# A Conformer block in one fp32 kernel: LayerNorm and the last two channel chunks by token halves, and weights' loads issued from ScalarE

## The reference, cut to what matters

```python
def conformer_conv_module(h, w_pw1, b_pw1, w_dw, b_dw, ln_g, ln_b, w_pw2, b_pw2):
    a, g = jnp.split(h @ w_pw1 + b_pw1, 2, axis=-1)
    u = a * jax.nn.sigmoid(g)
    u = causal_depthwise_conv(u, w_dw) + b_dw        # 31 taps over tokens, per channel
    u = jax.nn.silu(layer_norm(u, ln_g, ln_b))       # mean and variance over the 1024 channels
    return u @ w_pw2 + b_pw2
...
h = h + rms_norm(m, norm_mix_post[layer])
```

## Time and profile before

| | us |
|---|---|
| median of 3 runs | 2382.27 (2381.09 to 2384.25) |
| the profiled execution's own time | 2383.93 |
| its span in the profile | 2382.1 |
| TensorE busy | 2320.1 |
| VectorE busy | 1330.0 |
| ScalarE busy | 875.6 |
| mean granted TensorE clock | 0.992 of 2.4 GHz |

### The profile page before, as it was taken

How to read it: one execution, slowest core, us unless ns; L and a number is a source line. 1 busy time by engine, 2 the same in 40 slices (tenths; PEclk the granted TensorE clock), 3 DMA queues, 4 the chain that set the end, 5 groups by cost and what they waited for, 6 DMA issues and landing times.

```text
span 2382.1 us, 36397 instructions
## 1 busy us (share of the span) xinstructions
PE 2320.1 (97%) x14188; PEld 1959.3 (82%) x14188; DVE 1330.0 (56%) x1934; ACT 875.6 (37%) x1337; POOL 3.3 (0%) x5
## 2 busy tenths in 40 slices
PE   9999999999998999999999999999999989999998
PEld 7788888889876888888988877888888777888888
DVE  6564754522757564542366575666633885766523
ACT  6444422222424532222342364333322674333322
POOL 0000000000000000000000000000000000000000
PEclk9999999999998999999999999999999999999999
DMA  4112233222374232332232112223222202223222
GB/s 159 62 63 89 80 125 97 97 97 81 108 166 92 71 106 97 97 97 98 89 104 82 55 64 71 97 97 96 96 93 94 73 28 89 97 97 97 96 91 87
DMA packets 82604, 218.70 MB, mean 92 GB/s; under 512 B 10944, under 2 KB 31808, under 8 KB 82496
## 3 DMA queue, kind: packets, MB, share of 16 engines
q1 hardware_dynamic: 77472, 215.05, 28.6%
q10 hardware_dynamic: 5024, 2.10, 0.3%
HBM read 212.78 MB, written 4.34 MB: 91 GB/s over the span
## 4 chain that ended last, share of the span: by engine, by line
PE 82%; DVE 10%; ACT 5%; issue 2%; DMA 1%; SPq 0%; ACTq 0%; DVEq 0%
PE bank L459 23%; PE bank L461 23%; PE bank L460 23%; PE bank L659 2%; PE bank L658 2%; PE bank L660 2%; DVE w_lo L1596 2%; ACT ds L1533 1%; ACT w_hi L1076 1%; DVE m L1652 1%; DVE acc L1625 1%; DVE h L1657 1%; DVE small L2248 1%; PE bank L799 1%; DVE ds L2267 1%
## 5 line engine op out<-in xcount | busy, mean ns | idle before, releaser
L459 PE MATMUL bank<-u_hi,w_hi 128*128 128x512 f32 (+1 forms) x2090 | 798.1, 382 | 13.9 <-DVE w_lo L1596 6.3
L1076 ACT ACTIVATE w_hi<-raw 128x1024 fp32r<-128x1024 f32 x378 | 400.0, 1059 | 1083.6 <-PE bank L461 945.0
L460 PE MATMUL bank<-u_lo,w_hi 128*128 128x512 f32 (+1 forms) x2090 | 787.8, 377 | 0.0
L461 PE MATMUL bank<-u_hi,w_lo 128*128 128x512 f32 (+1 forms) x2090 | 787.5, 377 | 0.0
L1596 DVE TENSOR_TENSOR w_lo<-raw,w_hi 128x1024 fp32r<-128x1024 f32 x378 | 461.3, 1221 | 399.3 <-ACT w_hi L1076 398.8
L459 PEld LDWEIGHTS bank<-u_hi,w_hi 128*128 128x128 f32 x2090 | 394.1, 189 | 94.8 <-DVE w_lo L1596 7.1
L461 PEld LDWEIGHTS bank<-u_hi,w_lo 128*128 128x128 f32 x2090 | 394.1, 189 | 72.6
L460 PEld LDWEIGHTS bank<-u_lo,w_hi 128*128 128x128 f32 x2090 | 394.3, 189 | 71.3 <-issue 1.2
L459 PE MATMUL bank<-hid_hi,w_hi 128*128 (+1 forms) x440 | 173.4, 394 | 0.0
L461 PE MATMUL bank<-hid_hi,w_lo 128*128 (+1 forms) x440 | 172.5, 392 | 0.0
L460 PE MATMUL bank<-hid_lo,w_hi 128*128 (+1 forms) x440 | 170.8, 388 | 0.0
(11 more groups left out here) (301 smaller groups left out, 2491.5 us busy)
## 6 DMA issues: line engine op xcount, KB each, us to landing
raw<-weights_dram SPq DMA_DIRECT2D x378, 512.0 KB, 3.5
bz<-gated_dram SPq DMA_DIRECT2D x32, 268.0 KB, 5.1
gated_dram<-bz SPq DMA_DIRECT2D x8, 274.0 KB, 2.5
h<-x_t_dram SPq DMA_DIRECT2D x8, 256.0 KB, 6.3
out_dram<-m SPq DMA_DIRECT2D x4, 256.0 KB, 2.3
out_dram<-m ACTq DMA_DIRECT2D x4, 256.0 KB, 2.5
cmask<-masks_dram ACTq DMA_DIRECT2D x4, 224.0 KB, 3.9
ap<-select_dram SPq DMA_DIRECT2D x1, 512.0 KB, 8.7
```

What stands on the lines that cost most here:

```text
L459: pe.matmul(out, wh, xh, start=start, stop=False)
L460: pe.matmul(out, wh, xl, start=False, stop=False)
L461: return pe.matmul(out, wl, xh, start=False, stop=stop)
L1076: act.activation(w_hi[:, j, :], raw[:, j, :], ACT.Copy).then_inc(hi_ready, 1)
```

## The change

- `conformer_order`: chunks 6 and 7 (`WHOLE` = 6 whole chunks before them) are cut into token halves. Their four slots become eight `part` items (half 0 of slots 12 to 15, then half 1), and gating, exchange, convolution and spread run on "pieces": 0 to 5 are whole chunks, 6 and 7 the first halves of chunks 6 and 7, 8 and 9 the second.
- LayerNorm (sums, variance, root, centring, scaling, SiLU, low part) is done for half 0 and then for half 1, on pairs of chunks. SiLU's second result goes back to `by`; `by_lo` takes the place of `u_lo`.
- `first_outs`: for half 0 slots 0, 1 and 2 of b_out side by side, then slot 3; for half 1 slots 0 and 1 side by side, then 2 and 3. The spread and convolution of the last pieces stand between the pairs of half 0. 18 empty products before half 1, none before half 0.
- The loads of b_in slots 7 to 15 and of b_out slots 0 to 3 are issued from ScalarE's queue (`load_over`, `slot_next`); SyncE keeps b_in slots up to 6 and the exchanges.
- In `halved_out` of layer b, high and low parts of the slots come four ahead instead of three.

The diff, cut to its core:

```diff
+def piece(p):
+    if p < WHOLE:
+        return p, None
+    return WHOLE + p % 2, (p - WHOLE) // 2
...
     return items + [
+        ("part", 0), ("part", 1), ("gated", 6), ("conv", 4), ("spread", 3),
+        ("part", 2), ("part", 3), ("gated", 7), ("conv", 5), ("spread", 4),
+        ("part", 4), ("part", 5), ("gated", 8), ("conv", 6), ("spread", 5), ("conv", 7), ("spread", 6),
+        ("part", 6), ("spread", 7), ("part", 7), ("gated", 9),
+    ]
...
 # SyncE
-            for s in range(first - first % RING, first + RING):
+            for s in range(first - first % RING, first + RING + 2):
                 load_next(s)
-            for c in range(KC):
-                for s in (first + RING + 2 * c, first + RING + 2 * c + 1):
-                    load_next(s)
-                shift_gated(c)
+            shift_gated(0)
+            load_next(first + RING + 2)
+            for p in range(1, PIECES):
+                shift_gated(p)
...
 # TensorE
             pe.wait_ge(shift_ready, 1)
...
-            keep_awake(bank[0], 20)
-            halved_out("b_post", "b_out", by_hi, by_lo, normed_input("b_ln"), high_input("b_ln"))
+            norm_sums(0)
+            depthwise(WHOLE + 2)
+            pe.wait_ge(b_evac, 2 * PIECES)
+            first_outs(0, last_pieces)
+            norm_sums(1)
+            keep_awake(bank[6], 18)
+            first_outs(1, lambda pair: None)
+            halved_out("b_post", "b_out", by_hi, by_lo)
...
+            def first_outs(half, between):
+                s, t, side = SLOT["b_out"], tokens(half), 2 if half else 3
+                pe.wait_ge(w_ready, s + side)
+                for k in range(KC):
+                    if k % 2 == 0:
+                        pe.wait_ge(u_ready, SPLIT["b_ln"] + PAIRS * half + k // 2 + 1)
+                    for n in range(side):
+                        j = (s + n) % RING
+                        last = product(bank[n][:, t], weight(w_hi, j, k), weight(w_lo, j, k), by_hi[:, k, t], by_lo[:, k, t],
+                                       k == 0, k == KC - 1)
...
+                for n in range(side, 4):
+                    last = half_chunk(s + n, half, bank[n][:, t], by_hi, by_lo)
...
+            def last_pieces(pair):
+                if pair == 0: spread(WHOLE + 2)
+                elif pair == 2: depthwise(WHOLE + 3)
+                elif pair == 3: spread(WHOLE + 3)
...
 # ScalarE
+            def load_over(s):
+                j = s % RING
+                act.wait_ge(slot_done, s + 1)
+                act.dma_start(raw[:, j, :], weights[s + RING]).then_inc(raw_landed[j], 16)
+            def slot_next(s):
+                load_over(s)
+                high_part(s + AHEAD)
...
                 elif what == "part" and n == 7:
+                    load_over(SLOT["b_in"] + 2 * WHOLE + 2)
                 elif what == "gated":
...
+                    elif n == WHOLE + 2:
+                        load_over(SLOT["b_in"] + 2 * WHOLE)
+                        load_over(SLOT["b_in"] + 2 * WHOLE + 1)
+                    elif n == WHOLE + 3:
+                        load_over(SLOT["b_in"] + 2 * WHOLE + 3)
+                        high_part(SLOT["b_out"] + 2)
...
+            layer_root(0)
+            keep_piece(WHOLE + 2)
+            for pair in range(PAIRS):
+                silu_pair(0, pair)
+                if pair == 1:
+                    high_part(SLOT["b_out"] + 3)
+            keep_piece(WHOLE + 3)
+            square_made(WHOLE + 2)
+            square_made(WHOLE + 3)
+            layer_root(1)
+            for pair in range(PAIRS):
+                silu_pair(1, pair)
...
 # VectorE
+            layer_norm(0)
+            shifted(WHOLE + 2)
+            shifted(WHOLE + 3)
+            layer_norm(1)
```

More of the change, by code:

```diff
@@ L554, in post_sums, with halved_out @@
                 pe.matmul(to, ones[:, :], acc[:, tokens(half)], start=True, stop=True).then_inc(sum_full, 1)
[L556 to L561 removed]
+            def halved_out(stat, part, xh, xl):
+                s = SLOT[part]
                 for n in range(4):
@@ L781, in _, with depthwise @@
             pe.wait_ge(z_ready, 4)
-            halved_out("a_post", "a_out", acat_hi, acat_lo, fox_ready)
+            two_chunks(SLOT["a_out"], bank[0:2], acat_hi, acat_lo, fox_ready)
+            for n in range(2, 4):
+                chunk(SLOT["a_out"] + n, 0, bank[n][:, :], acat_hi, acat_lo)
+            halved_out("a_post", "a_out", acat_hi, acat_lo)
             feed_forward("a")
             halved_in("a_fpost", SLOT["b_in"])
-            def depthwise(c):
-                b = c % CONV_RING
-                out = bank[5 + c % 2]
+            def depthwise(p):
+                c, half = piece(p)
+                first, n = phase_columns(half)
+                b, out = c % CONV_RING, bank[5 + p % 2]
@@ L1351, in _, with silu_pair @@
+            def silu_pair(half, pair):
+                act.wait_ge(yn_ready, PAIRS * half + pair + 1)
+                for to, done in ((by_hi, uh_ready), (by, ut_ready)):
+                    for c in (2 * pair, 2 * pair + 1):
+                        ins = act.activation(to[:, c, tokens(half)], by[:, c, tokens(half)], ACT.Silu,
+                                             bias=col("ln_b", c), scale=col("ln_g", c))
+                    ins.then_inc(done, 1)
             for what, n in B_ITEMS:
@@ L1352, in _ @@
                 if what == "slot" and n % 2 == 0 and n >= 3:
-                    slot_over(SLOT["b_in"] + n)
+                    slot_next(SLOT["b_in"] + n)
+                elif what == "part" and n == 0:
+                    high_part(SLOT["b_in"] + 2 * WHOLE + 3)
+                elif what == "part" and n == 7:
+                    load_over(SLOT["b_in"] + 2 * WHOLE + 2)
                 elif what == "gated":
+                    c, half = piece(n)
+                    gate = ba[:, c % 2, 1, piece_tokens(half)]
@@ L1977, in _ @@
                         tap_blocks(n // 2 - 1)
+                elif what == "part":
+                    half, at = n // 4, n % 4
+                    slot, t = SLOT["b_in"] + 2 * WHOLE + at, tokens(half)
+                    if half:
+                        dve.wait_ge(slot_done, slot + 1)
+                    else:
+                        dve.wait_ge(part_full, at + 1)
+                        dve.wait_ge(bz_ready, WHOLE - 1 + at // 2)
+                    dve.tensor_tensor(ba[:, at // 2, at % 2, t], bank[at][:, t], rs[:, t], ALU.mult).then_inc(b_evac, 1)
+                    if n == 1:
+                        low_part(SLOT["b_in"] + 2 * WHOLE + 3)
+                    elif n in (0, 2, 4):
+                        tap_blocks(WHOLE - 1 + n // 2)
                 elif what == "gated":
+                    c, half = piece(n)
+                    at, cols = phase_columns(half)
                     if n >= 2:
```

290 lines of the change are left out of this document (172 added, 118 removed).

## The result

The changed kernel takes 2387.8 us in the median of 19 runs (2384.5 to 2393.5), the kernel before 2382.1 in the median of 20 (2380.1 to 2386.0). A twentieth run of the changed kernel took 5951.3 us and is left out of its median. The ratio is 1.0022 with a 95% interval of 1.0016 to 1.0028, and the medians lie **5.7 us** apart: the change is slower, by little and clear of noise. The forecast was 2379.0 with a range that ended at 2386.

The account below looks back on a forecast made before the run. TensorE, busy 97% of the span, was taken as the bound, leaving only idle or half-clock time to win. Early part -5.5 and tail +2.2 summed to -3.3 us, giving 2379.0 us from the median 2382.3; range 2371.5 to 2386.

Parts of the forecast that it names:

- Early part, forecast -5.5: Up to convolution 3: loads on ScalarE's queue shorten the waits before convolution 0 and spread 0; 5.5 us gained, bounds 3.5 to 6.6.
- The term charged with 1 us: Early part: slot 7's load beside chunk 0's exchange can hold back slot 6's load and ScalarE's order; 1 us lost.
- So the gain keeps: After the early part, up to 707.6 us: both kernels are bound by TensorE, so the 5.5 us gained stay.
- Rival (b): Early part: the loads gain nothing, as bytes and not order set the chain; only the tail's +2.2 is left, 2384.5; chance 0.12.
- Tail, forecast +2.2: From the end of convolution 3 to slot 4: 85.6 us against 83.4, so the tail loses 2.2 us.
- Cutting by tokens costs TensorE nothing there: Tail, token halves of slots: half a slot is 24 products of 0.113, 2.72 us, against 5.45 for a full one.
- One us of wait where spread 6 needs VectorE: Tail, before part 7 ends: TensorE waits 1 us at spread 6 for VectorE's shifted values.
- The idle time ahead of the first pair, put down to slot 18's load,: Tail, LayerNorm of half 0: ScalarE's chain stands behind slot 18's late load, so TensorE idles 8 us.
- 1.1 us of wait for the weights of slots 4 and 5: End of the tail: only two halves (5.4 us) cover these weights' loads; 1.1 us lost in two waits.
- From slot 4 on nothing changes: Behind the tail: no change; ScalarE reaches the first pair 0.5 us late, hidden by the stage's sums.
- (c): Output slots' weights land late, 8.8 us instead of 3.5, at the first u and slot 4: +6, 2388; chance 0.10.
- (a): Both parts gain: half SiLUs cost half, no wait at slot 4, clock back sooner; 2375; chance 0.36.

Follow-up runs that it names:

- experiment 5: Kernel before with the weights' loads on ScalarE's queue, but b_out slot 3's issued by SyncE behind chunk 7's exchange: 2379.3 us, ratio 0.9982.
- experiment 8: Kernel before with b_in slots 12 to 15 each computed as two token halves in a row: 2384.7 us, ratio 1.0004.
- Experiment 3: Changed kernel with the loads of b_out slots 0 to 3 back on SyncE, issued as buffers come free: 2388.4 us, ratio 1.0020.
- experiment 6: Changed kernel with 24 empty products between convolution 8 and the first output slots' first product: 2385.1 us, ratio 1.0007.
- experiment 4: Kernel before with a delay of nine empty products (2.1 us) after output slot 3: 2385.6 us, ratio 1.0013.
- experiment 9: Kernel before with empty products (7, 15, 15) in three later waits of TensorE: 2382.6 us, ratio 0.9997.
- experiment 10: Changed kernel with empty products (7, 15, 15) in three later waits of TensorE: 2386.8 us, ratio 1.0014.
- experiment 2: Changed kernel with all weights' loads back on SyncE in the order of before (the halves alone): 2390.8 us, ratio 1.0034.
- experiment 7: Changed kernel with nine empty products (2.1 us) ahead of the second halves of output slots 6 and 7: 2386.9 us, ratio 1.0013.
- experiment 12: Changed kernel with empty products in every longer wait, three later ones and four in the stage: 2386.7 us, ratio 1.0017.

## Why the prediction was wrong

**Early part, forecast -5.5.** Right in mechanism and size: -5.2 at convolution 3. Copy of convolution 0 at 661.05 (forecast 660.3), slot 8's high part without a wait for its load, no fall of the clock behind spread 0. The term charged with 1 us was 2: slot 6's high part waited for its load until 651.79 (649.75 before) and sigmoid 2 came at 659.48 (657.5). "So the gain keeps" is said up to 707.6, and there it held. But the sum then carried the whole of it through the tail, and the gain has first to pass the exchange of chunk 7: in the kernel of loads alone 5.0 us became 3.2 at convolution 7, where the load of b_out slot 3 stands in front of the store (experiment 5), and 2.9 in the median. Rival (b) falls: the order of the queue was worth microseconds, as the wait of SyncE for its store in rows 4 had suggested.

**Tail, forecast +2.2; this is where the prediction failed.** Counted in us from the end of convolution 3, forecast and changed kernel:

| | forecast | measured |
|---|---|---|
| part 7 ends | 35.7 | 38.5 |
| convolution 8 ends | 39.8 | 42.7 |
| first product of half 0 | 47.9 | 49.0 |
| half 0 of slots 0 to 3 done | 63.9 | 66.0 |
| first product of half 1 | 71.7 | 74.7 |
| slots 0 to 3 done | 84.5 | 87.8 |

- *"Cutting by tokens costs TensorE nothing there"* is the step that failed first. A half slot was priced with 24 x 0.113 from b_out's rows; on b_in they are 0.120 apart, in this kernel and in experiment 8, and a slot's two halves take 5.94 us (702.32 to 708.26), four slots 23.8 instead of 21.8. The row nearest in form was taken, not one of the same stage: b_in's own first halves stood in the trace of before with 0.120 (from 614.34 on). On b_out the 0.113 was not kept either: 0.119, an estimated 0.5 us for the 96 products of half 0.
- *One us of wait where spread 6 needs VectorE* was 1.9: 1.03 for VectorE, and 0.90 after its first four records, for which the trace names no releaser. That, the halves and small change make part 7 late by 2.8.
- *The idle time ahead of the first pair, put down to slot 18's load,* was 6.3 us, not 8, and has another cause: part 7, its evacuation and the sigmoid, then ScalarE's serial order. Experiment 3 took the load away and gained nothing. So 1.8 us of the lateness (2.9 at convolution 8, 1.1 here) was made good by luck, by an error of the other sign.
- *The clock behind it, 2.3 us,* came as 1.8 (pair 0 in 4.1 instead of 2.3). In this the forecast was right, and in experiment 6 pair 0 took 2.3 again.
- *First u 5.3 us after the sums* was 6.0. The pairs follow 1.96 us apart, as forecast: SiLU sets the second half's pace.
- *1.1 us of wait for the weights of slots 4 and 5* came in size and not in kind: the wait is 0.3 (at 793.47), and the rest up to 801 lies in the products, 0.119 us apart instead of 0.113, and in slower first products of a slot.
- The half convolutions (1.55) and spreads (0.72) came as forecast. 96 records in 1.55 us are 16 ns each. The 25 ns from start to start that the Trainium skill ("TensorE: Matmul & The Clock Gate", "Wait — 56ns, not 53.3ns?") states as a floor would make them 2.4 us, an estimate; the measurement decides.

From the first product on, 1.0 us more is lost up to the end of half 0, 0.9 from there to half 1's first product and 0.3 up to the end of slot 3. The tail was +5.5 in the traces (4.4 and 1.1) where +2.2 was forecast.

**Left out: the rest of the program.** "From slot 4 on nothing changes" is true of the instructions and not of the time: behind 801 the changed kernel's trace loses 3.6 us more. That this belongs to the change is not shown. The trace of experiment 6, whose code is the changed kernel's behind 801, went from 0.6 behind it to 3.0 ahead of it in the same three waits, and their clocks differ between equal code in experiment 4 as well; the medians of experiments 9 and 10 leave 1.5 us, within noise. On the other side, the profiled execution of before was itself 2.3 us behind an equal one at slot 3 (experiment 4), so the tail of the halves looked better against it than it is: alone they cost 7.9 us in medians.

**The rivals.** (c) gave the number, 2388, and the sign, by a mechanism that did not happen: the output slots' weights were not late. It had 0.10, since I tied "slower" to that single wait and did not price plain added work and added waits on TensorE's path. (a) fails in its first term: SiLU pairs at 1.96.

**What stays open.** How deep the clock falls behind the later waits differs from trace to trace (experiments 4 and 6); what decides it is not explained. The changed kernel itself was measured in one set of runs and not again on the chips of its variants (experiments 2, 3, 6, 7, 10 and 12), so a difference of 2 us between these and it can be the chip's. Nor was it tried to halve the chunks and leave LayerNorm whole, or to leave `by_lo` in its buffer, so how the 4.2 us divide was read from the trace alone.

## What to carry to other kernels

Work cut into pieces fills a wait only if the new pieces do not make a serial chain twice. Here the table loads, the variance, the SiLU pairs and the restart of TensorE ran once per half, and 8.8 us of idle time became 10.8. When TensorE is busy 97% of the time, price such a cut by its added work first, with rows of the same stage, and ask of every load moved to a second queue which small store it now runs beside. Before a delay is used to test a theory, look for a wait behind it that can swallow it. Where a few microseconds decide, compare medians: the clock alone moved one trace by some 2 us.

## What the runs showed of the hardware that I had not expected

- Keeping the clock up bought little here: with all longer waits filled the mean clock was 0.998 of full instead of 0.993, and the median just 0.9 us lower than in experiment 5, within noise. Most of the low clock must then have fallen into time that was not TensorE's to win; where, was not traced.
- The same three waits were followed by clocks of 0.89, 0.83 and 0.86 in one trace of the kernel before and of 1.00, 0.66 and 0.86 in one with equal code there. One pair of traces can't price them.
- Products of 256 columns, of the same shape and type, came 0.120 us apart on b_in, 0.113 and 0.118 within one stage of b_out, and 0.119 on b_out in the changed kernel.
- A store of 274 KB took 2.2 to 2.3 us to the next queue entry at chunk 7 with no load of another queue started just before it, and 2.4 to 3.7 us (chunks 4 to 7 of experiment 1) with a 512 KB load started 2 us earlier on ScalarE's queue.
